# State-space parameters of a head made during the head before it, and those of the first head during the input's loads

## What is computed

```python
h = rmsnorm(x, norm_mix_pre[i])
proj = h @ w_in[i]
q, k, v, gate, u = jnp.split(proj, [...], axis=-1)
...
y_ret = head_groupnorm(retention_chunkwise(qh, kh, vh), ret_gn_gain[i])
y_ret = silu(gate) * y_ret

def s5_scan(u, lam_re, lam_im, log_dt, b_re, b_im, c_re, c_im, d_skip):
    lam = lax.complex(jnp.minimum(lam_re, -1e-4), lam_im)
    dt = jnp.exp(log_dt)[:, None]
    lam_bar = jnp.exp(lam * dt)
    b_bar = ((lam_bar - 1.0) / lam)[:, :, None] * b_c
    bu = jnp.einsum('blgc,gpc->blgp', uf, b_bar)
    ...   # states: x <- lam_bar * x + bu
    y = jnp.real(jnp.einsum('blgp,gcp->blgc', states, c_c)) + d_skip * uf
```

## Time and profile before

| | us |
|---|---|
| median of three runs | 3223.57 (3221.07 to 3224.68) |
| the profiled execution, its time | 3225.02 |
| its span in the profile | 3223.2 |
| TensorE busy | 2934.8 (91%) |
| VectorE busy | 1496.0 (46%) |
| ScalarE busy | 620.4 (19%) |
| GpSimd busy | 963.8 (30%) |
| TensorE's mean granted clock | 0.93 of 2.4 GHz |
| from the start to the last product of `phase1` | 543.2 |

### The profile page before, as it was taken

One profiled execution on the slowest core, in us unless ns is written; L12 is line 12 of the kernel. 1 busy time (PEld: TensorE's weight loads), 2 busy tenths in 40 slices (PEclk: granted clock), 3 DMA queues, 4 the chain that ended last, 5 costly groups with the idle time before them and its releaser, 6 DMA issues. The chain is left out here.

```text
span 3223.2 us, 35641 instructions
## 1 busy us (share of the span) xinstructions
PE 2934.8 (91%) x14110; PEld 2434.1 (76%) x14110; DVE 1496.0 (46%) x1816; ACT 620.4 (19%) x991; POOL 963.8 (30%) x515
## 2 busy tenths in 40 slices
PE   4987976899999999998789699888999999999997
PEld 4766765788888888886677477677887788888886
DVE  7355453266322222237565597575427522222247
ACT  3212212232100011112222000453212111111011
POOL 1111101354433333344122133000254533333343
PEclk7978978999999999998789799999998999999998
DMA  3121121323222222223101034214132211111122
GB/s 127 52 58 51 45 60 67 115 80 100 85 65 65 65 65 72 72 87 97 55 21 39 26 110 125 93 53 163 33 105 92 72 53 52 46 46 52 46 65 98
DMA packets 89217, 231.28 MB, mean 72 GB/s; under 512 B 27600, under 2 KB 30928, under 8 KB 89104
## 3 DMA queue, kind: packets, MB, share of 16 engines
q1 hardware_dynamic: 52528, 173.72, 16.9%
q10 hardware_dynamic: 36576, 56.01, 5.6%
HBM read 199.16 MB, written 29.36 MB: 71 GB/s over the span
## 5 line engine op out<-in xcount | busy, mean ns | idle before, releaser
L194 POOL CAST w_hi<-w_raw 128x1024 fp32r<-128x1024 f32 x254 | 274.2, 1080 | 2197.0 <-PE ps L207 2184.2
L203 PE MATMUL ps<-a_hi,w_hi 128*128 128x512 f32 x2080 | 702.7, 404 | 45.5 <-PEq L2469 18.8
L196 POOL TENSOR_TENSOR w_lo<-w_raw,w_hi 128x1024 fp32r<-128x1024 f32 x254 | 686.5, 2703 | 20.3
L205 PE MATMUL ps<-a_lo,w_hi 128*128 128x512 f32 x2080 | 689.1, 397 | 0.0
L207 PE MATMUL ps<-a_hi,w_lo 128*128 128x512 f32 x2080 | 687.3, 396 | 0.0
L203 PEld LDWEIGHTS ps<-a_hi,w_hi 128*128 128x128 f32 x2080 | 397.9, 194 | 133.0 <-issue 29.1
L205 PEld LDWEIGHTS ps<-a_lo,w_hi 128*128 128x128 f32 x2080 | 401.0, 193 | 85.0
L207 PEld LDWEIGHTS ps<-a_hi,w_lo 128*128 128x128 f32 x2080 | 399.9, 192 | 86.3
L205 PE MATMUL ps<-g_b,w_hi 128*128 128x512 f32 x1216 | 414.9, 397 | 0.0
L203 PE MATMUL ps<-g_b,w_hi 128*128 128x512 f32 x1088 | 365.5, 398 | 30.3 <-DVE g_b L1205 20.8
L207 PE MATMUL ps<-g_b,w_lo 128*128 128x512 f32 x1088 | 361.5, 394 | 0.0
(11 more groups left out here) (400 smaller groups left out, 3088.0 us busy)
## 6 DMA issues: line engine op xcount, KB each, us to landing
w_raw<-in_wstream SPq DMA_DIRECT2D x254, 512.0 KB, 3.6
ada_w<-in_ada_w ACTq DMA_DIRECT2D x50, 512.0 KB, 3.6
y_by_token<-y ACTq DMA_DIRECT2D x12, 512.0 KB, 2.9
tmp_b<-mixer_out SPq DMA_DIRECT2D x8, 512.0 KB, 3.3
x_res_b<-in_xT SPq DMA_DIRECT2D x2, 2048.0 KB, 12.2
x_block<-x_res_b SPq DMA_DIRECT2D x16, 256.0 KB, 3.2
z_rows<-ada_w ACTq DMA_DIRECT2D x8, 512.0 KB, 2.7
u_rows<-pad ACTq DMA_DIRECT2D x8, 512.0 KB, 4.6
```

Source lines behind the costliest of these rows:

```text
L194: pool.tensor_copy(k.w_hi[:, s, :], k.w_raw[:, s, :]).then_inc(k.w_high, 1)
L196: pool.tensor_tensor(k.w_lo[:, s, :], k.w_raw[:, s, :], k.w_hi[:, s, :].bitcast(F32), ALU.subtract).then_inc(k.w_split, 1)
L203: pe.matmul(o, w_hi, a_hi[:, c], start=first, stop=False)
L205: pe.matmul(o, w_hi, a_lo[:, c], start=False, stop=False)
```

## The change

- VectorE's work on parameters is cut into functions. `parameters(i + 1)` (up to `bb`) stands behind the rope of K of head i; `state_inputs(i + 1)` (`hs`) behind V times `rstd`, ahead of the state scan. `state_outputs(i)` (`gg`) and `rotations(i)` (`rot`, `decay8`) stay in head i, behind U times `rstd`.
- Those of head 0: `parameters(0)` stands ahead of the input's chain; its `hs` in two halves, before and behind the reciprocal of the norm.
- On ScalarE `parameters_act(i + 1)` stands behind the eight transfers to `mT`, and these moved from ahead of `halves_swapped(K_)` to behind `u_grp`. The load of `prm` waits for `gg_ready` instead. For head 0 it stands ahead of the reads of x; the Silu of c moved behind the square root.
- On TensorE `K_ROWS` moved from behind `HT_IM` to behind `ADA3`, that is, behind tile K. The PSUM regions of `ADA2`, `ADA3` follow from that.
- The scaling of `cosr` and `sinr` moved from the prologue to behind head 0's `gg`.
- The hardware loops of ScalarE and VectorE are written out; the last load of `prm` is dropped.

```diff
-        (ADA0, ADA1, HT_RE, HT_IM, K_ROWS, ADA2, ADA3, U_BLOCKS, ...
+        (ADA0, ADA1, HT_RE, HT_IM, ADA2, ADA3, K_ROWS, U_BLOCKS, ...
...
+                ada(ADA2, 2)
+                tile(K_)
+                ada(ADA3, 3)
                 job(K_ROWS)
-
                 pe.wait_ge(gg_ready, i + 1)
-                pe.sem_inc(rows_begin, 1)
...
-                ada(ADA2, 2)
-                tile(K_)
-                ada(ADA3, 3)
                 job(U_BLOCKS)
...
+            def parameters_act(i):
+                act.wait_ge(prm_in, 16 * (i + 1))
+                act.activation(sm[:, 0, :], prm[:, ...], ACT.Exp).then_inc(dt_ready, 1)
+                act.wait_ge(mag_ready, i + 1)
+                ...
+                act.wait_ge(ang_ready, i + 1)
+                ...
+            parameters_act(0)
             act.wait_ge(const_in, 32)
...
                 ada(ADA2, 2)
-                act.wait_ge(rows_ready, i + 1)
-                for t in range(STEP):
-                    act.dma_start(mT[...], k_rows[...]).then_inc(mT_in, 16)
-                act.dma_start(prm[:, :], ...).then_inc(prm_in, 16)
+                if i + 1 < HEADS:
+                    act.wait_ge(gg_ready, i + 1)
+                    act.dma_start(prm[:, :], d.prm[i + 1, :, :]).then_inc(prm_in, 16)
                 halves_swapped(K_, 1)
...
                 act.activation(u_grp[...], Xf[0], ACT.Copy).then_inc(k.aux_free[0], 1)
+                act.wait_ge(rows_ready, i + 1)
+                for t in range(STEP):
+                    act.dma_start(mT[...], k_rows[...]).then_inc(mT_in, 16)
+                if i + 1 < HEADS:
+                    parameters_act(i + 1)
                 act.wait_ge(kT_ready, i + 1)
                 halves_swapped(Q_, 2)
...
-            with act.Fori(0, HEADS // 2) as jj:
+            for jj in range(HEADS // 2):
...
+            parameters(0)
+            dve.wait_ge(const_in, 32)
+            for t in range(KT):
+                ...   # the input's chain, as before
+            state_inputs(0, range(0, GT // 2))
+            dve.wait_ge(h_split, KT)
+            dve.wait_ge(root_done, 1)
+            dve.reciprocal(rcol[:, :], col[:, :]).then_inc(inv_done, 1)
+            state_inputs(0, range(GT // 2, GT))
...
                 rope(K_, 1, kT, kT_ready)
+                if i + 1 < HEADS:
+                    parameters(i + 1)
...
                 tt(vT[:, :], pair[s], rstd[:, :], ALU.mult).then_inc(k.pair_free[s], 1)
+                if i + 1 < HEADS:
+                    state_inputs(i + 1, range(GT))
 
                 job(STATES)
```

More of the change, by code:

```diff
@@ L89 @@
 IDENT, CENTER, TRI_LE, TRI_GE, TRI_GT, TRI_LT = range(6)
-STEP_LINKS = 328
 P1_TILES = HEADS * 5
@@ L288, in phase1 @@
         J = 20
-        (ADA0, ADA1, HT_RE, HT_IM, K_ROWS, ADA2, ADA3, U_BLOCKS, U_GROUPS, STATES, K_TOK, V_TOK, KV, SSM_Y, SCORES, SSM_T, RET_Y, CENTRED,
+        (ADA0, ADA1, HT_RE, HT_IM, ADA2, ADA3, K_ROWS, U_BLOCKS, U_GROUPS, STATES, K_TOK, V_TOK, KV, SSM_Y, SCORES, SSM_T, RET_Y, CENTRED,
          VARIANCE, RSTD) = range(J)
@@ L534, in step @@
                 ada(ADA0, 0)
[L535 to L542, removed]
                 ada(ADA1, 1)
@@ L621, in _ @@
             ch.link(dve.memset(rot[:, 0, :, 0], 1.0))
[L622 to L645, removed]
             def product(out, a, b, n, shape, conj=False):
@@ L660, in product, with prm_of, small, parameters @@
                 return tt(out[1], x, y, ALU.subtract if conj else ALU.add)
-            def step(jj, half):
-                i = 2 * jj + half
-                def prm_of(name, cols=None):
-                    ap = prm[:, PRM[name][0]:PRM[name][1]]
-                    return ap if cols is None else ap.rearrange("p (g c) -> p g c", c=cols)
-                def job(j):
-                    dve.wait_ge(k.aux_done, i * J + j + 1)
-                def small(j):
-                    return sm[:, j, :]
-                dt, lr, a, m1, m8, num, den, fr, fi, s1, s2 = (small(j) for j in (0, 1, 2, 3, 4, 5, 6, 7, 8, 9, 10))
+            def prm_of(name, cols=None):
+                ap = prm[:, PRM[name][0]:PRM[name][1]]
+                return ap if cols is None else ap.rearrange("p (g c) -> p g c", c=cols)
+            def small(j):
+                return sm[:, j, :]
+            dt, lr, a, m1, m8, num, den, fr, fi, s1, s2 = (small(j) for j in (0, 1, 2, 3, 4, 5, 6, 7, 8, 9, 10))
+            def parameters(i):
                 dve.wait_ge(prm_in, 16 * (i + 1))
@@ L718, in step, with state_inputs @@
                                 [prm_of("bre", GROUP_CH), prm_of("bim", GROUP_CH)], n, (GT, GROUP_CH)))
-                for g in range(GT):
+            def state_inputs(i, gs):
+                for g in gs:
                     last = product([hs[:, r, g, :, :] for r in range(2)],
@@ L725, in step, with state_outputs @@
                         ch.link(last)
-                last.then_inc(hs_ready, 1)
-                dve.wait_ge(hs_ready, i + 1)
+                    else:
+                        last.then_inc(hs_ready, 1)
+                        dve.wait_ge(hs_ready, i + 1)
+            def state_outputs(i):
                 for g in range(GT):
@@ L742, in step, with job @@
                                     [bc(x[:, j + 1, :], 2, w) for x in (cs, sn)], GT * w, (GT, w)))
+            parameters(0)
+            dve.wait_ge(const_in, 32)
+            for t in range(KT):
+                g = VEC["mix_pre"][0] + t
+                dve.wait_ge(x_in[t % XB], 16 * (t // XB + 1))
+                dve.wait_ge(h_high, t + 1)
+                stt(out=h_lo[:, t, :], in0=x_bufs[t % XB][:, :], scalar=k.vecs[:, g:g + 1],
+                    in1=h_hi[:, t, :].bitcast(F32), op0=ALU.mult, op1=ALU.subtract).then_inc(h_split, 1)
+                if t == 0:
+                    dve.wait_ge(x_sq, 1)
+                    dve.sem_inc(x_sum, 1)
+                elif t < KT - 1:
+                    dve.wait_ge(x_sq, t + 1)
+                    dve.wait_ge(x_sum, t)
+                    tt(yc[:, :], yc[:, :], (kT, qT)[t % 2][:, :], ALU.add).then_inc(x_sum, 1)
+            state_inputs(0, range(0, GT // 2))
[3 more added lines that the diff above has]
+            state_inputs(0, range(GT // 2, GT))
+            dve.wait_ge(rstd_row, 1)
+            dve.tensor_copy(rstd[:, :], Xf[1]).then_inc(rope_scaled, 1)
+            dve.wait_ge(rope_scaled, 1)
+            def step(jj, half):
+                i = 2 * jj + half
+                def job(j):
+                    dve.wait_ge(k.aux_done, i * J + j + 1)
                 dve.wait_ge(k.tile_done, i * tiles + U_ + 1)
@@ L817, in step @@
                 tt(yc[:, :], yc[:, :], vT[:, :], ALU.mult).then_inc(ret_ready, 1)
-            with dve.Fori(0, HEADS // 2) as jj:
-                ch.enter(jj, STEP_LINKS)
+            for jj in range(HEADS // 2):
                 step(jj, 0)
                 step(jj, 1)
-                ch.leave(HEADS // 2)
 class Work:
```

31 lines of the change are left out of this document (21 added, 10 removed).

## The result

| | median of four runs, us | lowest to highest |
|---|---|---|
| before | 3222.32 | 3216.89 to 3224.68 |
| with the change | 3197.15 | 3191.28 to 3201.73 |

The ratio is 0.9922, with a 95% interval of 0.9908 to 0.9937: 25.2 us gained at the medians, where 29.5 were predicted, and 3197.15 us where 3194.1 stood. The profiled execution of the changed kernel took 3191.28 us, the shortest of its four. Inside `phase1` the two traces differ by 25.1 us (the last product ends at 543.15 before, at 518.02 after); their spans differ by 33.7. The other 8.6 us arise in later stages, which the change doesn't touch: the profiled execution before took 2.7 us more than its median, that of the changed kernel 5.9 us less, which is the same 8.6. So I explain the 25.1 and leave the 8.6 out.

The account below looks back on a forecast made before the run. TensorE, busy 91% of the span, was taken as the bound, its idle time as the gain. 64.8 - 5.6 - 4.5 = 54.7 us, less 25.2, gave 29.5 gained: 3223.57 - 29.5 = 3194.1 us, range 3168 to 3210.

Parts of the forecast that it names:

- The waits for `hs` and `gg` go, `ada_w` is late next.: TensorE between `ADA1` and `ADA2`: 58.2 us of waits go, `ada_w` takes 3.9 a head; 64.8 us gained.
- `ADA2` and tile K stay at the low clock.: TensorE behind the `ada_w` load: clock stays low as before, nothing gained; if it held, 12.6 us.
- `K_ROWS`.: TensorE behind tile K: runs at full clock in 1.8 us, costing 1.4 us a head, 5.6 us in all.
- The input's chain.: VectorE's prologue: head 0's parameters stand ahead, first `a_lo` at 15.2 us; 4.5 us lost.
- The new wait.: `SSM_Y` on TensorE waits for VectorE's scan, 5.9 us in each of heads 0 to 2.
- the two causes that the prediction named: Ahead of VectorE's scan: parameters kept waiting by ScalarE's eight transfers (5.61 us), and `hs` (9.9 us).
- The third stall: VectorE's state scan: GpSimd's split behind tile G blocks it, 2.9 us; without it the wait is 3.0.
- The clock behind that wait.: TensorE after the `xp` wait: `SSM_Y` and what follows lose 2.5 us, in each of three heads.
- Slower through written-out loops.: Rival, 3%: VectorE's program arrives late in stalls of 1.84 us; seven a head give 3233 us.
- A longer wait: Rival, 11%: `xp` wait 8.7 us, prologue loss 6.8, perhaps `K_ROWS` at low clock; 3203 to 3214 us.

Follow-up runs that it names:

- e4: Changed kernel with head 0's parameters cut in two, the second half behind the norm's reciprocal, `hs` behind the norm's rows; 3197.09 us.
- e1: Changed kernel with `hs` of the next head moved from ahead of the state scan to behind the multiplication that makes `sT`; 3158.81 us.
- e2: Changed kernel with ScalarE's `parameters_act(i + 1)` ahead of the eight transfers to `mT` instead of behind them; 3164.84 us.
- e3: Changed kernel with five unused 128x512 products on TensorE ahead of `SSM_Y`'s wait for `xp` in heads 0 to 2; 3178.48 us.
- e6: Kernel before with only `K_ROWS` moved behind tile K and `ADA3`, and the `mT` transfers and `prm` load behind `u_grp`; 3188.56 us.
- e5: Kernel before with only the hardware loops of ScalarE and VectorE in `phase1` written out; 3217.44 us.
- e9_tail: Changed kernel plus `parameters_act` before `mT` transfers, `hs` behind `sT`, cut prologue, second `ada_w` buffer, unused wide products before `VARIANCE` and `RSTD` waits; 3133.40 us.

## Why the prediction was right, and where it was off

**Direction, size and range** hold: 3197.15 against 3194.1, in 3168 to 3210. The steps:

- *The waits for `hs` and `gg` go, `ada_w` is late next.* Right: 65.3 us for 64.8. `ADA2` starts 3.5 to 3.9 us after `ADA1`'s end, as issue and landing said. The transposes took 1.07 us in heads 1 to 3 and not 1.94, the clock being still up, which made the wait behind them longer and changed nothing else.
- *`ADA2` and tile K stay at the low clock.* Right for all but 2.0 us.
- *`K_ROWS`.* 5.4 us for 5.6. It takes 1.93 us at full clock, as half of the earlier trace rows.
- *The input's chain.* 4.4 us for 4.5, by parts that differ: the first `a_lo` came at 20.43, not 15.2, as GpSimd's two first splits fell on the last parameter instructions. In return the chain behind ran without their slowing, and the sums started at 35.75 for 36. e4 confirmed the cause by taking it away: `ADA2` of head 0 came 6.0 us earlier, of which 2.1 were left at the end of `phase1`.
- *The new wait.* Right in place, cause and number: three of 5.05, 5.16 and 4.67 us for 5.9. `xp` came 0.7 us earlier than counted; e1 and e2 each remove the wait by one of the two causes that the prediction named. The third stall, which the page "SBUF — State Buffer" of the Trainium skill, section "Who interferes with whom", made likely, is there: the two scans took 3.13 us in place of 2.48 and the multiply behind them 2.65 in place of 0.69. GpSimd lost too: its cast lasted 1.57 in place of 1.04 us and its subtraction 3.13 in place of 2.34. In order of time these are the cast, the second scan (from 122.57), the subtraction and the multiply. Each started while one of the other engine ran, which had 0.7, 0.8, 1.0 and 2.1 us left, and each became 0.5, 0.65, 0.8 and 2.0 us longer. The trace agrees with the exclusive lock of that section of the Trainium skill, which whoever issues first holds for its whole instruction: the two sides stood still in turn. Beside the parameters, where GpSimd's instructions had started first (97.02 and 98.14, against 97.03 and 98.18), VectorE alone lost: 1.04 and 2.36 us for instructions of 0.16.
- *The clock behind that wait.* **This term was mis-sized.** It read "`SSM_Y` and what follows lose the 2.5 us that tile K loses". Measured, `SSM_Y` loses 6.6 us (15.0 for 8.4) and `SCORES` 1.7 (3.78 for 2.05), 8.3 together, and the whole stretch to the next `ADA0` 25.6 us in three heads for 7.5. A price was taken from a stretch of 128x512 products and put on one of 128x128 and 64-row products, in which the clock did not come back. e3 measured this loss by itself. With this term right and the others as they stood, the sum would have been 11.4 us and the forecast 3212, outside its range. What saved it was luck, above all a gain I had at zero: the clock was back sooner at the head's end (1.00 from 168 to 172 us, where it was 0.50 before), so `ADA0` and U of heads 1 and 2 gained some 4 us each, 9.0 together with head 3. No run ties that gain to the change: e6, with neither the early parameters nor the `xp` wait, has it in heads 2 and 3 (16.4, 12.8, 13.0 us), and e4, with both, in head 2 only (16.4, 12.7, 16.6).
- *Slower through written-out loops.* e5 finds nothing of it.
- *A slip.* A longer wait, 11 to 20 us worse than 3194.1, is 3205 to 3214, where the prediction has 3203. Nothing rests on it.

Open: what makes the clock stay low through `SSM_Y` and rise in a tile; and why the tile U of some heads runs at full clock and of others not (11.2, 11.2 and 13.3 us in heads 1 to 3 of the changed kernel).

## What to carry over

When work moves into an engine's idle time, look at what stands behind it in that engine's queue and at the queues of other engines that it waits for: 24 instructions of `hs` ahead of the scan cost 38 us within `phase1`, and the same work behind `sT` cost nothing. Try each part of such a change alone, as the smallest (`K_ROWS` behind tile K) brought more than the whole (3188.56 against 3197.15 us). A wait of TensorE has a second price, the clock of what follows, and it must be read from a stretch of the same kind of products; if the wait must stay, a few wide unused products in it give that part back.

## What the runs showed of the hardware that I had not expected

- After 5 us idle, TensorE's clock stayed at 1.2 GHz over 20 us with TensorE busy for 18.4 of them, in narrow products. With five 128x512 products in the gap it stayed at 2.4 GHz through the same work.
- One such product (two instructions) in each of two gaps of about 1 us kept the clock at 2.4 GHz over the end of three heads of four (e9_tail: `RSTD` 2.05, 2.05, 3.39, 2.05 us; without them 3.28, 3.04, 2.66, 3.58).
- Where VectorE's scans met GpSimd's split, both lost in turn: each instruction that started while one of the other engine ran became longer by nearly what that one had left (VectorE 3.13 and 2.65 us for 2.48 and 0.69, GpSimd 1.57 and 3.13 for 1.04 and 2.34).
- Eight small transfers hold ScalarE's queue for 5.3 us, and its next activation with them.
- A wait for two semaphores was put down to "issue" (5.05 us) until it was under a microsecond.
